# Modulation of the second layer of a hybrid encoder: from eight row blocks ahead of the attention to eighths of columns inside it

## The reference

```python
cond = silu(c)
for i in range(2):
    mod = cond @ ada_w[i] + ada_b[i]             # 1024 x 3072
    shift, scale, gate = split(mod, 3)
    h = x * (1.0 + scale) + shift
    y = attention(h) if i == 0 else ssd(h)
    x = layer_norm(ALPHA * x + gate * y)
```

## Time and profile before

| | us |
|---|---|
| median of 3 runs | 2226.59 |
| the three runs | 2218.74, 2226.59, 2232.44 |
| the profiled execution, its time | 2223.36 |
| its span, first to last instruction | 2221.6 |
| around the span | 1.8 |
| mean granted TensorE clock | 0.987 |

### The profile page before, as it was taken

The page is one execution under the profiler, slowest core; times in us unless marked ns, Lnnn a source line. Parts: engine busy times, 40 slices in busy tenths (PEclk is TensorE's granted clock), DMA queues, the critical chain, the costliest instruction groups (busy, mean ns, idle before and its releaser), DMA issues.

```text
span 2221.6 us, 32885 instructions
## 1 busy us (share of the span) xinstructions
PE 2113.5 (95%) x11583; PEld 1686.8 (76%) x11583; DVE 1053.3 (47%) x2242; ACT 948.0 (43%) x2354; POOL 849.7 (38%) x444
## 2 busy tenths in 40 slices
PE   4999999999999999999999989899999989999997
PEld 3768888887888888878786777677777777777776
DVE  6722222222222222232223576688588588467553
ACT  3223333334334333343435245565565555475220
POOL 0211141231411414114124164466466366385463
PEclk9989999999999999999999999999999999999998
DMA  9701121211212112112122332454354354266331
GB/s 359 263 25 39 41 68 38 70 39 39 61 37 64 44 39 70 38 41 67 39 59 67 118 133 69 130 153 149 106 159 146 106 155 145 99 192 222 139 112 57
DMA packets 89629, 222.11 MB, mean 100 GB/s; under 512 B 16644, under 2 KB 34692, under 8 KB 86920
## 3 DMA queue, kind: packets, MB, share of 16 engines
q1 hardware_dynamic: 89480, 219.98, 31.0%
HBM read 195.75 MB, written 24.19 MB: 99 GB/s over the span
## 4 chain that ended last, share of the span: by engine, by line
PE 65%; DVE 10%; issue 9%; POOL 8%; DMA 4%; ACT 3%; SPq 0%; POOLq 0%; DVEq 0%; ACTq 0%
PE pp L500 37%; PE pp_s L1895 5%; PE tp L532 3%; PE sp_ L522 3%; PE yo_p L2089 3%; PE op L592 2%; POOL trunk L1803 2%; PE pp_s L2089 2%; POOL rw L1793 2%; POOL xw L1786 2%; DVE stage_s L2498 2%; PE op L581 1%; DMA trunk<-in_ada_w 1%; DVE num_wide L1066 1%; POOL xd L1779 1%
## 5 line engine op out<-in xcount | busy, mean ns | idle before, releaser
L433 POOL TENSOR_TENSOR w_lo<-w_raw,w_hi 128x1024 fp32r<-128x1024 f32 x80 | 193.1, 2414 | 859.6 <-ACT w_hi L758 859.6
L500 PE MATMUL pp<-h_hi,w_hi 128*128 128x512 f32 x1264 | 501.9, 397 | 0.1
L500 PE MATMUL pp<-h_hi,w_lo 128*128 128x512 f32 x1264 | 493.4, 390 | 0.0
L500 PE MATMUL pp<-h_lo,w_hi 128*128 128x512 f32 x1264 | 492.8, 390 | 0.0
L1027 DVE COPY probT<-tp 128x512 f32<-128x512 f32 x160 | 103.2, 686 | 561.5 <-PE tp L532 561.5
L1895 PE MATMUL pp_s<-h_hi,w_hi_s 128*128 128x512 f32 x624 | 272.3, 436 | 21.1 <-DVE stage_s L2498 18.1
L500 PEld LDWEIGHTS pp<-h_hi,w_hi 128*128 128x128 f32 x1264 | 238.2, 188 | 51.5 <-issue 5.2
L500 PEld LDWEIGHTS pp<-h_hi,w_lo 128*128 128x128 f32 x1264 | 237.6, 188 | 50.8
L500 PEld LDWEIGHTS pp<-h_lo,w_hi 128*128 128x128 f32 x1264 | 238.0, 188 | 46.8
L819 ACT ACTIVATE prob<-prob,mz 128x256 f32<-128x256 f32 (+2 forms) x384 | 169.8, 444 | 205.5 <-DVE mz L1008 205.5
L1895 PE MATMUL pp_s<-h_hi,w_lo_s 128*128 128x512 f32 x624 | 247.2, 396 | 0.0
(11 more groups left out here) (448 smaller groups left out, 3587.3 us busy)
## 6 DMA issues: line engine op xcount, KB each, us to landing
w_raw<-in_a_w SPq DMA_DIRECT2D x80, 512.0 KB, 3.4
rw<-cum_rows SPq DMA_DIRECT2D x32, 1024.0 KB, 5.6
w_raw_s<-in_b_w SPq DMA_DIRECT2D x40, 512.0 KB, 3.5
ew<-exp_rows SPq DMA_DIRECT2D x64, 256.0 KB, 4.8
trunk<-in_ada_w SPq DMA_DIRECT2D x8, 1536.0 KB, 6.7
num_wide<-merge_rows SPq DMA_DIRECT2D x16, 768.0 KB, 8.3
yT_b<-trunk SPq DMA_DIRECT2D x32, 256.0 KB, 2.3
stage_s<-yT_b SPq DMA_DIRECT2D x16, 512.0 KB, 5.3
```

Source lines behind the costliest of these rows:

```text
L433: nc.gpsimd.tensor_tensor(w_lo[:, slot].rearrange("p k c -> p (k c)"), w_raw[:, slot].rearrange("p k c -> p (k c)"), w_hi[:, slot].rearran ...
L500: last = nc.tensor.matmul(pp[:, par, :], w[:, slot, k, :], keep[h][:, k, half * HALF:(half + 1) * HALF], start=(k == 0 and n == 0), stop=( ...
```

## The change

- `load_next(e)` now loads an eighth of the **columns** (384 of the 3072) of all eight row blocks, as two transfers of 768 KB into `n_rows` (the `wide` half of `num_wide`). Eighth 0 is loaded in the prologue after the first layer's gate blocks; eighth j+1 in pair j, where SP is about to load tile f == 8, behind a new wait for `y_done`.
- `weigh_next` sums the eight blocks of 384 columns on DVE into the first of them: all eight in the prologue for eighth 0; in the pairs four at the end of duo 7 and four at the end of duo 8 (there behind the copies of the transposed values).
- `next_sums` on PE: three column products. In the prologue before unit 11; in the pairs right behind the transpose of the statistics, into the same bank. `columns_next` on DVE copies the three columns to `mods[:, 1]`, right behind the copy of the statistics, and gives `t_free` the second of its two counts.
- Gone: the 16 column products and the 4 row products of the second layer, the waits for eight blocks of 3072 columns, and the 1 x 1 bias products of the first layer's gate (its bias is added by DVE as it copies the row).
- The second layer's gate is now eight columns as well. Its bias is loaded as columns, element by element (4 bytes each), at the end of the prologue; after the loop DVE adds the biases, and SP writes the gate columns to DRAM element by element, before the loads of the output projection's weights.

```diff
+                def load_next(e):
+                    for half in range(2):
+                        src = io["ada_w"][1, HALF * half:HALF * half + HALF, bass.ds(EIGHTH * e, EIGHTH)]
+                        sp.dma_start(n_rows[:, 4 * half:4 * half + 4, :],
+                                     src.rearrange("(k p) c -> p k c", p=P)).then_inc(n_in[half], 16)
...
-                for k in range(2):
-                    load_next(k)
                 sp.wait_ge(h_lo, KT)
-                for n in range(2):
-                    sp.dma_start(g_rows[n], io["ada_b"][:, n, 2 * D:3 * D]).then_inc(brow_in, 16)
+                sp.dma_start(g_row, io["ada_b"][:, 0, 2 * D:3 * D]).then_inc(brow_in, 16)
                 for k in range(2, KT):
                     load_gate(k)
...
+                load_next(0)
+                for n in range(4, 10):
+                    load_first(n)
+                sp.dma_start(bcol[:, 1, 2 * KT:3 * KT], io["ada_b"][0, 1, 2 * D:3 * D].rearrange("(k p) -> p k", p=P),
+                             allow_slow_non_contiguous=True).then_inc(b_in, 16)
...
                 with sp.Fori(0, PAIRS - 1) as j:
                     for f in range(4, 14):
+                        if f == 8:
+                            sp.wait_ge(y_done, j + 1)
+                            load_next(j + 1)
...
+                sp.wait_ge(n_set, 2)
+                sp.wait_ge(gate_out, 16)
+                sp.dma_start(io["gate_row"][1].rearrange("(k p) -> p k", p=P), mods[:, 1, 2 * KT:3 * KT],
+                             allow_slow_non_contiguous=True).then_inc(gate_out, 16)
                 for k in range(KT):
                     load_w_out(k)
...
+                def next_sums(par):
+                    for i in range(NE):
+                        last = nc.tensor.matmul(tp[:, par, P + i:P + i + 1], n_acc[:, i * P:(i + 1) * P], ones[:],
+                                                start=True, stop=True)
+                    return last
+                def transpose_stats_and_sum(j, at, par):
+                    pe.wait_ge(t_free, at + 1)
+                    nc.tensor.transpose(tp[:, par, 0:P], mz[:], ident[:])
+                    pe.wait_ge(n_used, KT * j + 2 * KT)
+                    next_sums(par).then_inc(t_full, 2)
...
                         pe.wait_ge(t_free, T0 + 2)
-                        column_products(tp[:, 0], n_acc, ncol_full)
-                        pe.wait_ge(gate_copied, 1)
-                        gate_products(1, n_acc[:, 2 * D:3 * D])
+                        next_sums(0).then_inc(ncol_full, 1)
                         scores(0, 0)
...
+                def weigh_next(e, ks):
+                    for k in ks:
+                        if k % 4 == 0:
+                            dve.wait_ge(n_in[k // 4], 16 * e + 16)
+                        if k == 0:
+                            ins = nc.vector.tensor_scalar(n_acc, n_acc, cond[:, 0:1], None, ALU.mult)
+                        else:
+                            dve.wait_ge(n_used, KT * e + k)
+                            ins = nc.vector.scalar_tensor_tensor(n_acc, n_rows[:, k, :], cond[:, k:k + 1], n_acc,
+                                                                 ALU.mult, ALU.add)
+                        ins.then_inc(n_used, 1)
+                def columns_next(e, par):
+                    return nc.vector.tensor_copy(mods[:, 1, bass.ds(NE * e, NE)], tp[:, par, P:P + NE])
...
                     if d == 9:
                         event(j, ("s", 0), table)
+                        if not last_pair:
+                            columns_next(j + 1, table[("s", 0)] % 2).then_inc(t_free, 1)
...
                     if d in V_AT and ("v", V_AT[d], 0) in table:
                         for half in range(2):
                             event(j, ("v", V_AT[d], half), table)
+                    if d in (7, 8) and not last_pair:
+                        weigh_next(j + 1, range(4 * (d - 7), 4 * (d - 7) + 4))
```

More of the change, by code:

```diff
@@ L170, in attention_phase @@
         g_acc, g_ring = nw[:, 0], [nw[:, 1], nw[:, 2]]
-        n_acc = nw[:, 3:6].rearrange("p a c -> p (a c)")
-        n_ring = [trunk[:, 3 * D * i:3 * D * (i + 1)] for i in range(2)]
-        g_rows = [trunk[0:1, (6 + i) * D:(7 + i) * D] for i in range(2)]
+        g_row = trunk[0:1, 6 * D:7 * D]
+        EIGHTH = 3 * D // 8
+        n_rows = nw[:, 3:6].rearrange("p a c -> p (a c)").rearrange("p (k c) -> p k c", k=KT)
+        n_acc = n_rows[:, 0, :]
+        NE = EIGHTH // P
         pp = ps("pp", [P, 2, HALF])
@@ L597, in values, with gate_products @@
                     last.then_inc(o_full, 1)
-                def gate_products(n, acc):
-                    pe.wait_ge(brow_in, 32)
+                def gate_products():
                     for half in range(2):
[L604 to L607, removed]
+                        last = nc.tensor.matmul(op[0:1, half, :], ones[:], g_acc[:, half * HALF:(half + 1) * HALF],
+                                                start=True, stop=True)
                     last.then_inc(gate_full, 1)
[L610 to L614, removed]
                 pe.wait_ge(ones_set, 1)
@@ L647, in _ @@
                         pe.wait_ge(g_used, KT)
[L648 removed]
+                        gate_products()
                     if un in (3, 9):
@@ L1026, in copy_t @@
                         src = tp[:, par, :]
-                    nc.vector.tensor_copy(dst, src).then_inc(t_free, 1 if ev[0] in "pv" else 2)
+                    nc.vector.tensor_copy(dst, src).then_inc(t_free, 2 if ev[0] == "e" or ev[0] == "s" and last_pair
+                                                             else 1)
                 def event(j, ev, table):
@@ L1067, in weigh_rows, with gate_row @@
                     ins.then_inc(used, 1)
[L1069 to L1077, removed]
+                def weigh_next(e, ks):
[11 more added lines that the diff above has]
+                    return nc.vector.tensor_copy(mods[:, 1, bass.ds(NE * e, NE)], tp[:, par, P:P + NE])
+                def gate_row():
+                    dve.wait_ge(gate_full, 1)
+                    dve.wait_ge(brow_in, 16)
+                    nc.vector.tensor_tensor(g_row, op[0:1].rearrange("p a b -> p (a b)"), g_row, ALU.add
+                                            ).then_inc(gate_copied, 1)
                 for k in range(KT - 1):
@@ L1091, in pair_columns @@
                     dve.wait_ge(col_full, i + 1)
-                    dst, b = (t.rearrange("p (s k) -> p s k", s=2)[:, :, 2 * i:2 * i + 2]
+                    dst, b = (t.rearrange("p (s k) -> p s k", s=3)[:, 0:2, 2 * i:2 * i + 2]
                               for t in (mods[:, 0, :], bcol[:, 0]))
@@ L1118, in _ @@
                     copy_t(("v", at // 2, at % 2), at, at % 2)
[L1119 to L1126, removed]
+                weigh_next(0, range(KT))
+                gate_row()
+                for at in range(2, T0):
+                    copy_t(("v", at // 2, at % 2), at, at % 2)
                 dve.wait_ge(ncol_full, 1)
-                columns(1, tp[:, 0, 0:2 * KT])
-                gate_row(1)
+                columns_next(0, 0).then_inc(n_set, 1)
                 ch0 = Chain(dve, v_step, 0)
@@ L1172, in _ @@
                 ch = Chain(dve, v_step, ch0.n + STEPS * (PAIRS - 1))
+                dve.wait_ge(t_free, T0 + NT * (PAIRS - 1) + 2)
+                dve.wait_ge(b_in, 48)
+                cm_.link(nc.vector.tensor_tensor(mods[:, 1, :], mods[:, 1, :], bcol[:, 1], ALU.add))
+                nc.vector.tensor_scalar(mods[:, 1, KT:2 * KT], mods[:, 1, KT:2 * KT], 1.0, None, ALU.add
+                                        ).then_inc(n_set, 1)
                 def y_rest(m):
@@ L1750, in _ @@
                 sp.wait_ge(o_lo_done, KO)
+                sp.wait_ge(first["gate_out"], 32)
                 for dst, src in ((gate_r, io["gate_row"]), (lng_r, io["ln_g"]), (lnb_r, io["ln_b"])):
```

42 lines of the change are left out of this document (12 added, 30 removed).

## The result

The changed kernel takes **2248.8 us** (median of 4, 2247.3 to 2251.2) against 2229.5 before on the same chip: ratio 1.0106, 95% interval 1.0074 to 1.0138. The forecast was 2217.9 us, 0.4% less, with the range up to 2231. The change makes the kernel 1.1% slower, so the forecast was wrong in sign. The profiled execution has a span of 2247.2 us, 25.6 more than before.

What follows compares the result with a forecast made beforehand. PE was taken to bound the kernel. Prologue -20.2 us and seven pairs at 1.65 us (+11.5) make -8.7 from a median of 2226.59: forecast 2217.9 us, range 2206 to 2231.

Steps and rivals of the forecast that it cites:

- What bounds the kernel: Whole kernel: PE is busy nearly everywhere, without idle in the pairs; other engines count only where they make PE late.
- Prologue, -20.2: Before unit 11: 17.1 us of work and waiting removed, 1.2 for the clock, 1.9 for first-layer bias products.
- Its rival: Prologue: something else holds PE before unit 11 and the clock falls as before; half the gain lost, 2228 us; chance 0.05.
- Products, 0.75 per pair: PE, behind the transpose of the statistics: six records of column products add 0.75 us per pair, bounds 0.65 and 1.3.
- The sums in duo 8, stall 0.9: Start of duo 9: four DVE sums delay the copy of the probabilities, so PE idles 0.9 us per pair.
- My upper bound, 0.7 us per operation: DVE's sums in duo 8: at 0.7 us each with 0.1 between, PE's stall is at most 1.6 us per pair.
- The clock: Duo 9, statistics: rival that PE's clock falls in every pair after idle, 4.5 us each, 2249 us; chance 0.06.
- 0.9 us safe: Duo 9: PE's idle of 0.9 us is too short for a fall; 3.7 us had one, 1.27 us none.
- the gate products at a clock of 1.00: First layer's prologue: 3.8 us of thin gate products were not followed by a clock fall, taken as evidence against one.
- Transfers, zero: Prologue end and after the loop: element-wise transfers of 1024 4-byte pieces cost nothing, covered by 14 and 20 us.
- SP's wait for `y_done`, `t_free`'s later count, the loads of 1.5 MB: SP and POOL in the pairs: all zero; without POOL's cover the later count would cost up to 2 us per pair.
- the upper bound of 2231: Whole kernel: upper end of the 8-in-10 range, from 2226.7 us for pairs giving back all, plus 4 us.

Runs made afterwards that it cites:

- run 6: Changed kernel with DVE's sums ahead of the value copies and the gate write later, but all loads, sums and products of the pairs removed: 2201.3 us, ratio 0.9889.
- run 2: Changed kernel with its sums in place, but POOL's split of tile f = 10 waits until DVE has copied the probabilities: 2220.5 us, ratio 0.9981.
- run 4: Changed kernel without the six records of column products in the seven pairs, loads and sums kept: 2242.9 us, ratio 1.0088.
- run 3: Changed kernel with the element-wise gate write issued behind the loads of the second block of output weights: 2245.2 us, ratio 1.0092.
- run 1: Changed kernel with the four sums of duo 8 ahead of the copies of the transposed values: 2212.5 us, ratio 0.9949.
- run 5: Changed kernel with duo 8's sums ahead of the value copies and the gate write behind the second block of output weights: 2209.5 us, ratio 0.9921.

## Why the prediction was wrong

- **What bounds the kernel**: right. PE has no slack in the pairs, and all that was found is a wait of PE, its clock or its products.
- **Prologue, -20.2**: right; -21.2 to the first pair, and 20.8 in run 6. Its rival is out.
- **Products, 0.75 per pair**: right in size, 0.66 at full clock (run 6); up to 1.0 with its seams in the changed kernel, mostly at the lower clock.
- **The sums in duo 8, stall 0.9**: this step failed. I took the duration of a sum by itself, 0.55 us (0.62 measured), and never asked what POOL does in that stretch. Its split begins there in every pair, and one of the four sums lasts as long as the split. My upper bound, 0.7 us per operation, excluded it. A row that I had put on record showed it: the same operation with 1024 columns at 1285 ns, with a maximum of 3336; I used the first number and not the last. In the trace of the kernel before that long one, too, stands beside a split:

```profile
67.74 2.39 POOL L433 TENSOR_TENSOR w_lo<-w_raw,w_hi 128x1024 fp32r<-128x1024 f32 x1 [9.41 <-ACT w_hi L758]
...
67.87 3.34 DVE L1066 SCALAR_TENSOR_TENSOR num_wide<-num_wide,cond 128x1024 f32<-128x1024 f32 x1 [1.08 <-DMA num_wide<-in_ada_w]
```

And at the place to which the sums were moved, behind the copies of the earlier trace rows, a split began at 263.67. Run 2 takes the split away and gets the 0.9 us.
- **The clock**: the rival had the right place and mechanism, at 0.06. It was priced at 4.5 us per pair, and it was 2.2, what the prologue had lost on the dense work and no more. I called 0.9 us safe, which it was in run 2; with 2.9 it was not. I had let the gate products at a clock of 1.00 speak against a fall; but they had no idle ahead of them, and run 4 shows that the idle is enough without products. This rival's time, 2249 us, is the measured one by luck: its clock is 16 us too dear over seven pairs, and it lacks the longer stall (14 us) and the last pair (6 us).
- **Transfers, zero**: this step failed too, by 5 to 6 us. I asked who is queued behind the element-wise write, and nobody in need was. The one it hurt was the broadcast issued just ahead of it. The rule of the Trainium skill that I quoted (DMA: Bandwidth & Descriptors, Rules for kernel authors), one descriptor per element, spoke against the change here, and I had said that nothing hangs on it. The windows agree that such a transfer is dear per byte: the engines were busy at 0.83 for 6 us and moved 36 GB/s.
- **SP's wait for `y_done`, `t_free`'s later count, the loads of 1.5 MB**: zero, as forecast (run 6).
- **The arithmetic of the chances**: stall, clock and transfer were treated as rivals, one or the other. They aren't exclusive: the stall made the fall of the clock. By what was measured, the longer stall adds 14 us to the forecast, the clock 15 and the last pair 6. Each of them alone ends near the upper bound of 2231 or below it; together, 35 us, they end far above.

## What to carry to other kernels

Work that is moved into idle time of one engine must be looked up against what the other engines do at that minute: here four DVE operations that cost nothing 10 us earlier cost over 5 us per pair beside a GpSimd operation, in the stall and the clock behind it. Where a row of the same operation has a maximum far above its median, look at what ran beside the long one before pricing it. Where TensorE has no slack, a wait can cost more than its own length: behind 2.9 us here the clock took 2.2 us more. A transfer in many small pieces has to be checked against the transfers in flight ahead of it, not only against those behind it.

## What the runs showed of the hardware

- A scalar-tensor-tensor of 128 x 384 with both tensors in SBUF takes 0.62 us by itself. Begun 0.2 us after a GpSimd tensor-tensor of 2.37 us it takes 2.59. It ends 0.41 us behind that operation, which is its own length less 0.2. The one of 128 x 1024 in the kernel before (1.29 us by itself), begun 0.13 us after a split, ends 1.08 us behind it, again its own length less 0.2.
- In duo 9 the granted clock fell after 1.6 us of idle in six pairs of seven, in none after 0.93 us, and in all after 2.2 and 2.9 us. The one pair without a fall at 1.6 us, the second, had the same instructions and the same idle. In the output projection it fell once among idles of 0.88 us and less (run 3), and once stayed after one of 1.97 us (run 6).
- Falls after the same length of idle, 2.9 us, cost different amounts: the unit of 5.5 us behind them took 7.1 to 8.4.
- 1024 pieces of 4 bytes stretched a 768 KB broadcast that was issued 0.9 us ahead of them from about 8 to 15.3 us (14.8 in run 1, where the write stood at the same place; at most 9.4 with the write moved, in runs 3 and 5).
